# Byte offsets of seven weight places in on-chip memory, in a float32 encoder block

## The reference

```python
def swiglu(h, w_gate, w_up, w_down):
    return (jax.nn.silu(h @ w_gate) * (h @ w_up)) @ w_down

h = rms_norm(x, g_ffn1_pre)
x = x + 0.5 * rms_norm(swiglu(h, w_ffn1_gate, w_ffn1_up, w_ffn1_down), g_ffn1_post)
h = rms_norm(x, g_mix_pre)
proj = h @ w_in                     # attention q, k, v; retention q, k, v, g; two gates
merged = sigmoid(gate_sb) * (stick_breaking(q, k, v) @ w_proj_sb) \
       + sigmoid(gate_ret) * (retention(q, k, v, g) @ w_proj_ret)
x = x + rms_norm(merged @ w_out, g_mix_post)
h = rms_norm(x, g_ffn2_pre)
x = x + 0.5 * rms_norm(swiglu(h, w_ffn2_gate, w_ffn2_up, w_ffn2_down), g_ffn2_post)
```

## Time and profile before

| | us |
|---|---|
| median of 3 runs | 1366.22 (1366.1 to 1368.4) |
| the profiled execution | 1366.35 |
| its span, first to last instruction | 1364.3 |
| TensorE matmuls busy | 1349.2 (99% of the span) |
| TensorE weight loads busy | 1209.1 (89%) |
| VectorE busy | 1029.3 (75%) |
| ScalarE busy | 734.3 (54%) |
| GpSimd busy | 99.9 (7%) |

### The profile page before, as it was taken

The page is one execution under the profiler, slowest core; times in us unless marked ns, Lnnn a source line. Parts: engine busy times, 40 slices in busy tenths (PEclk is TensorE's granted clock), DMA queues, the critical chain, the costliest instruction groups (busy, mean ns, idle before and its releaser), DMA issues.

```text
span 1364.3 us, 22732 instructions
## 1 busy us (share of the span) xinstructions
PE 1349.2 (99%) x8668; PEld 1209.1 (89%) x8668; DVE 1029.3 (75%) x1124; ACT 734.3 (54%) x1008; POOL 99.9 (7%) x156
## 2 busy tenths in 40 slices
PE   8999999999999999999999999999999999999998
PEld 7999999999888888777778888799999999988886
DVE  7987888788988964667664334689788878888896
ACT  6554554555765743666653233555454455458663
POOL 0000000001330000322210000000000000025000
PEclk9999999999999999999999999999999999999999
DMA  6333332347994555212113345333333234399844
GB/s 209 109 92 109 123 108 82 117 123 248 197 202 155 191 179 139 77 48 63 47 47 93 93 122 189 106 100 113 113 123 108 80 120 123 112 284 198 177 139 154
DMA packets 152935, 177.71 MB, mean 130 GB/s; under 512 B 5552, under 2 KB 116400, under 8 KB 152752
## 3 DMA queue, kind: packets, MB, share of 16 engines
q1 hardware_dynamic: 139536, 151.54, 35.2%
q0 software_dynamic: 13056, 25.17, 10.2%
q10 hardware_dynamic: 288, 0.26, 0.1%
HBM read 170.66 MB, written 6.29 MB: 130 GB/s over the span
## 4 chain that ended last, share of the span: by engine, by line
PE 91%; DVE 4%; ACT 2%; DMA 1%; issue 1%; POOL 0%; SPq 0%; DVEq 0%; ACTq 0%; POOLq 0%
PE ps L797 14%; PE ps L800 14%; PE ps L799 14%; PE ps L898 8%; PE ps L899 7%; PE ps L900 7%; PE ps L730 6%; PE ps L732 5%; PE ps L731 5%; PE ps L737 2%; PE ps L738 2%; PE ps L739 2%; PE ps L1090 1%; DMA w_raw<-w_ffn_up 1%; PE ps L1045 1%
## 5 line engine op out<-in xcount | busy, mean ns | idle before, releaser
L797 PE MATMUL ps<-s_hi,u_hi 128*128 128x256 f32 x960 | 268.0, 279 | 1.5 <-DVE u_lo L1805 0.8
L800 PE MATMUL ps<-s_hi,u_lo 128*128 128x256 f32 x960 | 267.7, 279 | 0.0
L799 PE MATMUL ps<-s_lo,u_hi 128*128 128x256 f32 x960 | 267.7, 279 | 0.0
L797 PE MATMUL ps<-a_hi,u_hi 128*128 128x256 f32 x808 | 225.7, 279 | 1.1 <-DVE a_lo L1760 1.1
L800 PE MATMUL ps<-a_hi,u_lo 128*128 128x256 f32 x808 | 225.4, 279 | 0.0
L799 PE MATMUL ps<-a_lo,u_hi 128*128 128x256 f32 x808 | 225.3, 279 | 0.0
L1291 ACT ACTIVATE u_hi<-w_sum 128x1024 fp32r<-128x1024 f32 x120 | 124.0, 1057 | 173.0 <-DVE w_sum L1834 80.3
L797 PEld LDWEIGHTS ps<-s_hi,u_hi 128*128 128x128 f32 x960 | 180.5, 188 | 2.1 <-ACT m_c L1325 1.1
L799 PEld LDWEIGHTS ps<-s_lo,u_hi 128*128 128x128 f32 x960 | 180.5, 188 | 0.0
L800 PEld LDWEIGHTS ps<-s_hi,u_lo 128*128 128x128 f32 x960 | 180.5, 188 | 0.0
L898 PE MATMUL ps<-w_hi,l_hi 128*128 128x512 f32 x448 | 174.9, 390 | 0.1
(11 more groups left out here) (222 smaller groups left out, 2529.1 us busy)
## 6 DMA issues: line engine op xcount, KB each, us to landing
w_raw<-w_ffn_gate SPq DMA_DIRECT2D x64, 512.0 KB, 5.2
w_raw<-w_ffn_up SPq DMA_DIRECT2D x64, 512.0 KB, 4.7
d_sum<-w_ffn_down POOLq DMA_DIRECT2D x48, 512.0 KB, 12.3
w_raw<-w_in SPq DMA_DIRECT2D x44, 512.0 KB, 4.2
w_raw<-w_ffn_down SPq DMA_DIRECT2D x40, 512.0 KB, 4.2
d_sum<-w_ffn_down SPq DMA_DIRECT2D x16, 512.0 KB, 8.0
x_tok<-x SPq DMA_DIRECT2D x8, 512.0 KB, 6.0
d_m_raw<-w_ffn_down SPq DMA_DIRECT2D x8, 512.0 KB, 8.4
```

Source lines behind the costliest of these rows:

```text
L797: pe.matmul(o, wh, hi[:, k, :], start=first and f == 0 and k == 0, stop=False, skip_group_check=True)
L799: pe.matmul(o, wh, lo[:, k, :], start=False, stop=False, skip_group_check=True)
L800: mm = pe.matmul(o, wl, hi[:, k, :], start=False, stop=last and k == KH - 1, skip_group_check=True)
```

## The change

The constant 224 becomes seven numbers, one for each slot. They are odd multiples of 16, which the allocator doesn't take as a start; so the tile starts at the multiple of 32 below, is 4 elements (16 bytes) wider, and its first 4 elements are skipped.

```diff
-UP_OFF = 224
+UP_OFF = (48, 80, 112, 144, 176, 208, 240)
...
             at = raster + 2 * i * UNIT * 4
-            u_hi.append(place(f"u_hi{i}", [P, UNIT], F32R, at=at + UP_OFF)[0])
+            at += UP_OFF[i] // 32 * 32
+            pad = UP_OFF[i] % 32 // 4
+            u_hi.append(place(f"u_hi{i}", [P, UNIT + pad], F32R, at=at)[0][:, pad:])
             at += UNIT * 4
-            w_sum.append(place(f"w_sum{i}", [P, UNIT], at=at + UP_OFF)[0])
-            u_lo.append(place(f"u_lo{i}", [P, UNIT], F32R, at=at + UP_OFF)[0])
+            w_sum.append(place(f"w_sum{i}", [P, UNIT + pad], at=at)[0][:, pad:])
+            u_lo.append(place(f"u_lo{i}", [P, UNIT + pad], F32R, at=at)[0][:, pad:])
```

## The result

The changed kernel takes 1373.38 us (median of 4 runs, 1373.15 to 1373.52), the kernel before 1367.31 us (4 runs, 1366.1 to 1368.59). The ratio is 1.0047, 95% interval 1.0035 to 1.0059: slower by 0.47%. The forecast was 1372.0 us.

What follows compares the result with a forecast made beforehand. TensorE's gate and up matmuls were taken to bound the kernel. With all else at nothing, a mean shift of 1.07 ns by 5328 matmuls added 5.7 us to 1366.35, giving 1372.0 us, range 1350 to 1384.

Steps and rivals of the forecast that it cites:

- What bounds the kernel, and the multiplier: Gate and up stages: TensorE waits for nobody, 116.7 ns a matmul; 5328 matmuls make 1 ns of spacing worth 5.3 us.
- The cause: Gate and up matmuls: 119.6 ns in `b22`'s block at 0, 116.7 at 224, read as two accesses hindering each other by address.
- VectorE, ScalarE, DMAs at nothing: Tile writes and reads at odd multiples of 16 cost nothing; no DMA is added, removed or moved in its queue.
- The size: Gate and up matmuls: mean shift of 1.07 ns by 5328, +5.7 us, giving 1372.0 us.
- How the size was shared out: Seven gate and up slots: a straight line from 2.9 ns extra at 0 to none at 224; 48 gets a 0.79 share.
- the prediction's own last test: Gate and up blocks: the prediction is wrong in kind if per-slot times don't follow the distance from 0.
- the argument beside the line: Gate and up slots: 224 is one of the two best placed offsets seen, so seven others are more likely worse.
- The sign of the recorded weight loads: Gate and up stages: weight loads longer than 188 ns should go with the longer blocks.
- The rival of no change: Gate and up slots: only alignment with the moving tiles is bad, all seven cost what 224 costs; 1366.4 us, chance 0.26.
- The rival that odd multiples are better: Gate and up slots: odd multiples of 16 take the two reads apart; 1345.8 us if half of 7.7 ns went, chance 0.27.
- the 7.7 ns above the floor: Gate and up matmuls pay 116.7 ns against 109 ns, the fastest steady pace in the trace; gaining all is 41 us.
- The slowed VectorE: Gate and up stages: odd starts slow VectorE or ScalarE; 0.4 us more per large instruction gives 26 us, 1393 us, chance 0.02.

Runs made afterwards that it cites:

- the surveys: The changed kernel and four versions with other `UP_OFF` numbers (32 to 224, 256 to 448, 272 to 464, 40 to 136), those four at 1372.45 to 1374.60 us.

## Why the prediction was right, and where not

*What bounds the kernel, and the multiplier.* Right. The only thing that changed is the interval of 5328 matmuls, and 1.35 ns by 5328 gives the 7.1 us of the two spans.

*The cause: the weight load and the matmul that it overlaps hinder each other by their addresses' distance.* The prediction read it from two blocks and called it a reading. That the placement sets the rate is shown: seven offsets gave seven block times, and one offset for all slots gave one. Moving one moving tile by 96 bytes and no weights changed the product that reads it, 2.80 to 2.84 us a block, so both addresses count. That it is their distance alone fits, but rests on that one run; that the two reads meet in the memory is still inferred. The Trainium skill, SBUF — State Buffer, section "Who interferes with whom", says that TensorE has independent read ports for its two operands and never waits on anyone. The runs don't agree as far as these two reads go: the same instructions took 113.35 to 120.0 ns each, by placement and rhythm.

*VectorE, ScalarE, DMAs at nothing.* Right (1220 and 1057 ns, no new wait of TensorE). The other stages stayed as they were, as foretold: 882 matmuls in the first down stage's 196 us, 881 before.

*The size.* A mean shift of 1.07 ns was forecast, 1.35 was measured in the profile; +5.7 us against +7.2 there, and +6.1 between the medians; the median of before lies between its two levels. The time, 1373.38 us, is 1.4 us above the forecast.

*How the size was shared out.* This step was wrong, and by the prediction's own last test it makes the prediction wrong in kind: the per-slot times don't follow the distance from 0. The prediction drew a straight line from 0, dear, to 224, cheap, and foretold the longest block at 48. It was at 112 and 144; 48 cost half of what the line gave, 144 three times as much. There is no such line: over the 36 offsets of the surveys and of all at 0 the price goes up and down between 114.4 and 120.1 ns. That the line's mean, 1.07 ns, came near the measured 1.35 is luck. What was sound is the argument beside the line: 224 was among the two best placed offsets in sight, and seven other numbers would on average be worse. The four other surveys bear that out (1372.45 to 1374.60 us), and so the result was close to what seven arbitrary offsets cost. The sign of the recorded weight loads held in part: over pairs 4 to 15 of the first stage they take 189.0 and 189.6 ns at 112 and 144, the dearest slots, and 187.5 to 188.1 ns in the other five, but the block at 80 is longer than that at 48 with the shorter loads (187.7 against 188.1 ns).

*The rival of no change* fell with the seven unequal blocks. *The rival that odd multiples are better* fell in both parts: its sign, and parity as a cause, since all at 208 gives the time of all at 224, and seven even multiples give 1372.45 us. There was a reserve, though, if not by parity: of the 7.7 ns above the floor, 3.3 can be had, at 64. *The slowed VectorE* didn't occur.

*A step that was missing.* The prediction took one rate for one offset. Its own trace holds a second one: the first three blocks of the second feed-forward block, in column pair 0, have their weights at 224, as nearly all others, and run slower. The first matmul and the last of the third of them, in the kernel before:

```profile
891.42 0.28 PE L797 MATMUL ps<-a_hi,u_hi 128*128 128x256 f32 x1
...
894.13 0.28 PE L800 MATMUL ps<-a_hi,u_lo 128*128 128x256 f32 x1
```

That is 2.71 us for 23 intervals, 117.8 ns, where the blocks at 224 of the later pairs take 116.7. With all at 208 the second and the third of these blocks take 119.9 and 120.0 ns. By an estimate as above, 13 pairs of one stage at 117.8 in place of 116.7 ns are 1.1 ns by 2184, 2.4 us, about the step between the two levels of the kernel before (1366.2 and 1368.5 us). So these may well be rhythms too, but no profile shows its upper level, and two of its 51 runs beside the experiments (1367.1 and 1371.4 us) lie at neither level.

*Left open:* why 64 and 88 allow so short an interval, what a wait of TensorE does to the rhythm so that it changes at one and not at another, and whether the offset's price in the surveys is a price of the offset or of the rhythm that it happened to be in.

## What to carry to other kernels

When every matmul loads new weights and TensorE is never idle, the placement of the stationary tile against the moving one is a parameter to try: in this kernel it is worth some 2%, 1382 us with all at 0 and 1351 to 1357 us at the best. Survey it with several values in one run, reading each block's time from the starts in the timeline, but confirm the best alone and in many runs: a block's rate depends on what ran before it (192 took 113.3 ns and then 117.8 in one run), and a placement with two rhythms shows a median that hides two levels. An offset that is good in one stage must be tried anew in the next.

## What was not expected of the hardware

The same instruction stream at the same addresses and the same granted clock held 117.7 ns a matmul through one stage and 113.35 ns through the other, in one execution. The slow rhythm lasted about 297 us and 2520 matmuls. The fast one set in right behind a wait of TensorE of 0.71 us and lasted to the end of its stage. It can be steered to a degree: two blocks at other offsets before the blocks at 64 were followed by the fast rhythm in 28 of 30 column pairs of the profiled run, the two others being second pairs of a stage, with a wait of TensorE at the lead-in, and all five runs lie at one level. One block at 32 left the slow rhythm as it was in the one pair that shows it without a wait.
